# The first query products of finished token tiles placed at the end of the output projection's block, and the second query group's rounding with them

## The reference

```python
y = hybrid_mixer(h, ...)                       # ends in: merged @ w_out
x = x + gate1 * rms_norm(y, g_post_mix[l])
h = rms_norm(x, g_pre_ffn[l]) * (1.0 + scale2) + shift2
...
qry = (h @ w_query).reshape(T, P_HEADS, 2, P_HALF)          # T = 512, w_query is 1024 x 2048
scores = jnp.einsum("thcd,hcnd->thcn", qry, sub_keys)
s_top, i_top = lax.top_k(scores, P_TOPK)
```

## Time and profile before

| | us |
|---|---|
| three runs, median (lowest to highest) | 2040.17 (2038.8 to 2041.48) |
| the profiled execution | 2043.64 |
| its span, first to last instruction | 2041.9 |
| TensorE busy | 1950.5, 96% |
| VectorE busy | 1495.0, 73% |
| ScalarE busy | 720.0, 35% |
| GpSimd busy | 607.7, 30% |

### The profile page before, as it was taken

How to read it: one execution, slowest core, us unless ns; L and a number is a source line. 1 busy time by engine, 2 the same in 40 slices (tenths; PEclk the granted TensorE clock), 3 DMA queues, 4 the chain that set the end, 5 groups by cost and what they waited for, 6 DMA issues and landing times.

```text
span 2041.9 us, 27960 instructions
## 1 busy us (share of the span) xinstructions
PE 1950.5 (96%) x10317; PEld 1721.8 (84%) x10317; DVE 1495.0 (73%) x2721; ACT 720.0 (35%) x1324; POOL 607.7 (30%) x364
## 2 busy tenths in 40 slices
PE   5999998999999979999999999999999999999996
PEld 3889776889877868899999999999978888788885
DVE  5677545364475536777889999997688988788993
ACT  4010234010252243344443444444444444344442
POOL 0343402343203113101113732223433333343420
PEclk9999998999999989999999999999999999999998
DMA  6335411354212422257777688888999999999991
GB/s 249 103 104 185 165 51 40 100 202 144 62 42 76 151 83 75 74 171 252 232 225 256 222 314 305 305 303 308 411 379 394 396 396 397 396 397 396 391 346 68
DMA packets 230643, 468.00 MB, mean 229 GB/s; under 512 B 15576, under 2 KB 159120, under 8 KB 227728
## 3 DMA queue, kind: packets, MB, share of 16 engines
q1 hardware_dynamic: 193680, 332.54, 46.5%
q0 software_dynamic: 36864, 134.23, 17.4%
HBM read 412.19 MB, written 54.53 MB: 229 GB/s over the span
## 4 chain that ended last, share of the span: by engine, by line
PE 39%; DMA 10%; DVE 6%; issue 1%; ACT 1%; SPq 0%; POOL 0%; POOLq 0%; ACTq 0%; DVEq 0%
PE xin_ps_u L1946 23%; PE xin_out L1995 13%; DMA experts_hot<-act_scratch 8%; PE xin_out L1968 4%; DMA con_raw<-in_expert_u 1%; DVE over_v_vlo L2249 1%; DVE experts_acc L1765 1%; DVE experts_rows L1745 1%; DVE xin_wt L2246 1%; DVE in_ulo L2083 1%; DMA act_scratch<-in_act 0%; DVE xin_wlo L2251 0%; ACT in_uhi L2006 0%; SPq L1919 0%; DVE over_s_stage L2097 0%
## 5 line engine op out<-in xcount | busy, mean ns | idle before, releaser
L1946 PE MATMUL xin_ps_u<-con_h_hi,in_uhi 128*128 128x384 f32 x1024 | 348.0, 340 | 7.8 <-DVE in_ulo L2083 5.6
L1946 PE MATMUL xin_ps_u<-con_h_lo,in_uhi 128*128 128x384 f32 x1024 | 342.4, 334 | 0.0
L1946 PE MATMUL xin_ps_u<-con_h_hi,in_ulo 128*128 128x384 f32 x1024 | 342.4, 334 | 0.0
L1735 POOL DMA_INDIRECT experts_rows<-in_expert_rows,experts_idx x128 | 164.9, 1288 | 442.9 <-DVE experts_rows L1745 320.1
L1738 POOL DMA_INDIRECT experts_rows<-in_expert_v,experts_idx x128 | 201.9, 1578 | 313.7 <-DVE experts_acc L1765 297.3
L1995 PE MATMUL xin_out<-over_v_vhi,xin_whi 128*128 128x512 f32 x768 | 237.6, 391 | 8.6 <-DVE xin_wlo L2251 8.5
L476 POOL TENSOR_TENSOR weights_wlo<-con_raw,weights_whi 128x2048 fp32r<-128x2048 f32 x34 | 156.6, 4607 | 271.2 <-DVE weights_whi L537 271.2
L1995 PE MATMUL xin_out<-over_v_vlo,xin_whi 128*128 128x512 f32 x768 | 237.0, 390 | 0.0
L1995 PE MATMUL xin_out<-over_v_vhi,xin_wlo 128*128 128x512 f32 x768 | 236.8, 390 | 0.0
L2083 DVE TENSOR_TENSOR in_ulo<-con_raw,in_uhi 128x1024 fp32r<-128x1024 f32 x127 | 155.3, 1222 | 74.7 <-ACT in_uhi L2006 72.1
L1946 PEld LDWEIGHTS xin_ps_u<-con_h_hi,in_uhi 128*128 128x128 f32 x1024 | 192.4, 188 | 12.1 <-DVE in_ulo L2083 9.3
(11 more groups left out here) (330 smaller groups left out, 3819.1 us busy)
## 6 DMA issues: line engine op xcount, KB each, us to landing
con_raw<-in_expert_u SPq DMA_DIRECT2D x128, 512.0 KB, 5.1
con_raw<-in_expert_v SPq DMA_DIRECT2D x128, 512.0 KB
con_raw<-in_w_in SPq DMA_DIRECT2D x38, 1024.0 KB, 5.8
act_scratch<-in_act SPq DMA_DIRECT2D x128, 192.0 KB
experts_hot<-act_scratch SPq DMA_DIRECT2D x128, 192.0 KB
gate_scratch<-in_stage SPq DMA_DIRECT2D x12, 1024.0 KB
gate_scratch<-over_s_stage SPq DMA_DIRECT2D x12, 1024.0 KB
experts_hot<-gate_scratch SPq DMA_DIRECT2D x16, 768.0 KB
```

Of the source, the lines that this page charges most:

```text
L1735: pool.indirect_dma_start(out=self.rows[:, r % ROWS, 0:D], out_offset=None, in_=u_table, in_offset=at).then_inc(self.u_row_in[r % ROWS], 16)
L1946: mm = pe.matmul(ps_u[s % 2][:, 0:TD], a[s % 2][:, k, :], m[:, k, P:T], start=(i == 0), stop=(i == 3 * KD - 1))
```

## The change

Group 0 of the queries is cut by tokens. At the end of `finish_block`, TensorE computes both of its units for tiles 0 and 1 (256 tokens, `first_queries(slice(0, 2 * P))`) between the turns of tiles 2 and 3, and for tile 2 (128 tokens) behind the turn of tile 3. Only tile 3 (128 tokens) is left for `group(0)` in `query_block`. The two banks of PSUM go over from the one block to the other. Group 1 is rounded in `finish_block`, too: the high part by ScalarE in front of `modulate(3)`, the low part by GpSimd as its last instruction there; both are gone from `query_block`, whose counts of `w_hi` and `w_lo` are one lower, and the load of group 3 waits for nothing now.

```diff
@@ finish_block, gpsimd, behind the eight powers
+            pool.wait_ge(w_hi, 5)
+            pool.tensor_tensor(slots.wlo[1][:], raw[1][:], as_f32(slots.whi[1][:]), ALU.subtract).then_inc(query_lo, 1)
@@ finish_block, tensor
+            def first_queries(some):
+
+                for c in range(2):
+                    cs, i = slice(c * P, (c + 1) * P), 0
+                    for k in range(KD):
+                        for a, m in ((slots.whi, hi), (slots.whi, lo), (slots.wlo, hi)):
+                            pe.matmul(bank[c][:, some], a[0][:, k, cs], m[:, k, some], start=(i == 0), stop=(i == 3 * KD - 1))
+                            i += 1
+
             turn(2)
+            pe.wait_ge(w_lo, 4)
+            pe.wait_ge(low_done, 4)
+            for b in range(2):
+                pe.wait_ge(freed[b], U // 4)
+            first_queries(slice(0, 2 * P))
             turn(3)
+            pe.wait_ge(low_done, 6)
+            first_queries(slice(2 * P, 3 * P))
@@ finish_block, scalar
-                dst = w_hi_of[n] if n < 4 else slots.whi[0]
-                if n == 4:
-                    act.wait_ge(units, units_of.index((3, 0)) + 1)
+                dst = w_hi_of[n] if n < 4 else slots.whi[n - 4]
+                if n >= 4:
+                    act.wait_ge(units, units_of.index((3, n - 4)) + 1)
                 act.activation(dst[:], raw[n % 2][:], ACT.Copy).then_inc(w_hi, 1)
...
             modulate(2)
             square_tile(3)
+            split_hi(5)
             modulate(3)
@@ query_block, sync
-                wait(sp, w_lo, g - 2)
+                wait(sp, w_lo, g - 3)
...
-                sp.wait_ge(w_lo, PH - 2 + m // 2)
+                sp.wait_ge(w_lo, PH - 3 + m // 2)
@@ query_block, gpsimd
-            for g in range(1, PH):
-                pool.wait_ge(w_hi, g)
+            for g in range(2, PH):
+                pool.wait_ge(w_hi, g - 1)
@@ query_block, tensor
-                if g > 0:
-                    pe.wait_ge(w_lo, g)
+                if g > 1:
+                    pe.wait_ge(w_lo, g - 1)
+                some = slice(3 * P, T) if g == 0 else slice(0, T)
...
-                            mm = pe.matmul(bank[b][:], a[s][:, k, cs], m[:, k, :], start=(i == 0), stop=(i == 3 * KD - 1))
+                            mm = pe.matmul(bank[b][:, some], a[s][:, k, cs], m[:, k, some], start=(i == 0),
+                                           stop=(i == 3 * KD - 1))
@@ query_block, scalar
-                if g + 1 < PH:
+                if 0 < g < PH - 1:
```

More of the change, by code:

```diff
@@ L1235, in finish_block @@
              "stored"))
+        query_lo = al.sem("query_lo")
         pow_at = lambda kind, t: NORMS.index((kind, t)) + 1
@@ L1461, in _ @@
                         rounded(t)
+    return bank[0:2]
 class Consts:
@@ L1516, in mixer @@
         af.sb("m", [P, 2 * KD, T])
-        finish_block(nc, con, slots, A, m_hl, y, x_rows, late_w, x, x1, *hT)
+        return finish_block(nc, con, slots, A, m_hl, y, x_rows, late_w, x, x1, *hT)
 class Ring:
@@ L1597, with query_block @@
 PIECES, LATE_HEADS = 4, 2
-def query_block(nc, con, slots, ring, A, hT, qry, keys, rt, uhi, ulo, cut_hi, cut_lo):
+def query_block(nc, con, slots, ring, A, hT, qry, keys, rt, uhi, ulo, cut_hi, cut_lo, begun):
     with Alloc(nc, "query") as al:
@@ L1607, in query_block @@
         keys_t = al.sb("keys_t", [P, HC, NK])
-        bank = [al.ps(f"bank{i}", [P, T]) for i in range(4)]
+        begun_home = [al.ps(f"begun{i}", [P, T]) for i in range(2)]
+        bank = begun + [al.ps(f"bank{i}", [P, T]) for i in range(2)]
         ps = [al.ps(f"ps{i}", [P, 4, NK]) for i in range(4)]
@@ L2283, in _, with experts @@
                     dve.tensor_tensor(x[:, t + 1, half], x[:, t + 1, half], yg[m % 4][:], ALU.add).then_inc(dve_sum, 1)
-def experts(nc, con, slots, ring, A, hT, x1, acts, gmat, out):
+def experts(nc, con, slots, ring, A, hT, x1, acts, gmat, out, begun):
     with Alloc(nc, "over_s") as av:
@@ L2305, in experts @@
             qry = got.rows[:].rearrange("p a n -> p (a n)").rearrange("p (c t) -> p c t", t=T)
-            query_block(nc, con, slots, ring, A, hT, qry, hot[0:2], rt, uhi, ulo, cut_hi, cut_lo)
+            query_block(nc, con, slots, ring, A, hT, qry, hot[0:2], rt, uhi, ulo, cut_hi, cut_lo, begun)
             stage.append(stage1)
@@ L2327, in build_program @@
             head_block(nc, con, slots, A, A["x"].rearrange("b s d -> (b s) d"), *hT)
-            mixer(nc, con, slots, A, hT, x1)
+            begun = mixer(nc, con, slots, A, hT, x1)
         ring = Ring(al, slots)
-        experts(nc, con, slots, ring, A, hT, x1, acts, gmat, out.rearrange("b s d -> (b s) d"))
+        experts(nc, con, slots, ring, A, hT, x1, acts, gmat, out.rearrange("b s d -> (b s) d"), begun)
 NAMES = ["x", "c", "w_ada", "b_ada", "g_pre_mix", "g_post_mix", "g_pre_ffn", "g_post_ffn", "w_in", "b_if", "conv_w",
```

## The result

Five runs of each kernel, side by side on one chip: 2040.71 us before (2038.80 to 2043.27), 2049.49 us after (2047.08 to 2050.35). The ratio is 1.0040, 95% interval 1.0029 to 1.0052: slower by 8.2 us, 5.9 to 10.6. The forecast was 2050.6 and "slower".

A forecast was written before the change was run, and what follows sets the result against it. TensorE was taken to bound the kernel, with stops of 5.1 and 3.1 us and a lowered clock at the seam. 8.0 + 2.4 = 10.4 us slower, added to the median 2040.17, gave 2050.6; range 2037.5 to 2053.5.

The forecast's parts named there:

- Steps 1 and 2: Old block: 48 products of 256 columns take 5.8 us, to 747.1; then tile 3's turn at full clock, 1.9 us.
- The moved rounding: Old block: GpSimd's 4.6 us subtraction, ready at 746.85, gets in behind VectorE's tile 2 subtraction or cast, blocking VectorE until 751.6-752.0.
- step 3: Behind the turn of tile 3: TensorE waits for rounded tile 2, ready at 752.5 instead of 748.1.
- Step 4: Behind the turn of tile 3: TensorE stops from 749.0 to 752.5, some 3.4 us, and the clock falls.
- the stop at 1490: TensorE's stop of at least 3 us at 1490, which did not drop the clock; cited for the clock staying up.
- Steps 5 and 6: Tiles 2 and 3: 48 products each, 10.6 us at lower clock; query block 10.6 later, group 0's end 8.0 late.
- Step 7: Key transposes and group 1 start at the lower clock: 4.8 us of it cost 2.4 us.
- two records per narrow product: Rival: a 128-column product costs 0.236 us, 48 take 11.3; group 0 ends 11.8 us late, 2052.0; chance 0.13.
- Clock falls but rises within the narrow products: Rival: VectorE blocked, clock rises after 4.8 us within the 128-column products; 0.7 us late, 2040.9; chance 0.22.
- no block: Rival: GpSimd gets in only after 748.14, or not at VectorE's cost; 4.9 us sooner, 2035.3; chance 0.11.
- clock stays: Rival: VectorE blocked, but the clock stays up behind the stop; 1.6 us sooner, 2038.6; chance 0.09.
- hidden edits: Query block: group 3's early load behind the keys, costed at nothing; 3.6 us if transfers shared evenly and nothing hid it.

The follow-up runs named there:

- e1: The changed kernel with GpSimd's subtraction of group 1 and the load of group 3 back in the query block; -4.7 us against before, ratio 0.9972 to 0.9990.
- e2: The changed kernel with group 1's subtraction on VectorE behind its last rounding instead of on GpSimd; -4.8 us against before, ratio 0.9970 to 0.9990.
- e7: The changed kernel with GpSimd's subtraction of group 1 cut into four at the same place; -3.6 us against before, ratio 0.9969 to 0.9988.
- e3: The changed kernel with 15 unread 512-column products filling the stop behind the turn of tile 3; -1.8 us against before, ratio 0.9985 to 1.0003.
- e5: e4 with GpSimd's subtraction of group 1 back in the query block; -7.5 us against before, ratio 0.9945 to 0.9971.
- e8: The changed kernel with both of group 1's roundings back in the query block, only products moved; -5.3 us against before, ratio 0.9964 to 0.9986.
- e4: The changed kernel with tiles 2 and 3 done together as 256-column products in the query block; -3.0 us against before, ratio 0.9979 to 0.9996.
- e6: e1 with the keys' transposes moved between the two halves of group 1's products; -6.4 us against before, ratio 0.9953 to 0.9979.
- e9: e5 with the stop filled by 15 unread products and the keys' transposes between group 1's halves; -7.4 us against before, ratio 0.9952 to 0.9979.

## Why the prediction was right

By its steps, all counted from the turn of tile 2:

- **Steps 1 and 2** (first products, turn of tile 3): the turn started at 8.34 us, forecast 8.2, and took 1.95 at full clock. The 48 products of 256 columns took 5.83 us, 0.12 each.
- **The moved rounding and step 3**: GpSimd started 7.88 us behind the mark (forecast 7.9), got in at the end of the first of the two instructions named, and tile 2 was ready at 13.58 (forecast 13.6). e1, e2 and e7 show that it is this instruction and its length that does it.
- **Step 4**: a stop of 3.35 us (forecast 3.4), and the clock fell. The prediction assumed this. That the stop brings the fall is shown by e3 (stop filled, 1.00 throughout) and e5 (a stop of 3.6 us with no narrow products behind it, and the clock fell). But such a stop does not always do it, and the case against, the stop at 1490, was weaker than it looked: the same stop, 3.34 to 3.35 us long, stands in all eleven profiles, and behind it the clock fell in eight and stayed at 1.00 in three, the kernel before among them. In the changed kernel (stop from 1492.20 to 1495.55) it fell there, too:

```profile
1492.00:1495.00 3.00, 0.20 (x2) 0.00 (x0) 1.41 (x3) 1.84 (x3) 0.94 (x1) 1.00 1.03 408
1496.00:1498.00 2.00, 2.00 (x6) 1.54 (x6) 0.47 (x1) 0.81 (x1) 0.00 (x0) 0.50 1.04 419
```

- **Steps 5 and 6**: the narrow stream did not raise the clock. A narrow product at the lower level measured 0.214 us (48 in 10.28), not 0.22, and the clock fell only 1.7 us into the stream, so that some 15 of them still ran at 0.112. The block switch came 8.9 us later than before (forecast 10.6), the transposes of the keys 6.0 later (forecast 8.0). 15 x 0.108 + 81 x 0.006 is 2.1 us, which covers the miss of 2.0 at the transposes.
- **Step 7**: mis-sized. The clock came back at the end of the transposes, not 4.8 us after they began, so they cost 1.3 us more than before instead of 2.4. The sum is 6.0 + 1.3 = 7.3 where the prediction had 8.0 + 2.4 = 10.4; 7.3 is below its own bounds of 9.0 to 12.2, which had no place for a clock that falls late.
- **The total** was nearer (+8.8 by medians, +8.2 by the ratio, 5.9 to 10.6) than the sum, by scatter of the runs, not by merit.

The rivals: two records per narrow product are out (the trace has one record for each narrow product, and at full clock 16 of them in e1 start between 746.28 and 747.96, 0.112 us apart; the prediction had 0.115). Half as many columns go hardly faster than 256 (0.12). The page TensorE: Matmul & The Clock Gate (Trainium skill, LDWEIGHTS (loading the stationary operand)) gives a load's ns as its columns over 1.2, by which an estimate for 128 is 107 ns: the trace's 0.112 us per product at full clock stands near that (at the lower level it is 0.214), and far from the 81 ns per product that the same page has (Back-to-back issue gap), which the prediction turned down. "Clock falls but rises within the narrow products" fell with the changed kernel's own windows; "no block" and "clock stays" did too. Their prices held where an experiment made them true: e1 is "no block" (forecast 4.9 us faster, measured 4.7) and e3 is "clock stays up" (forecast 1.6 us faster, measured 1.8, with an interval that reaches no difference).

Of the hidden edits: the early load of group 3 behind the keys cost little, if anything. With it the wait for the keys ended 6.6 (e2), 6.0 (e3) and 6.4 us (e7) after the block start, with the old order 6.3 (e1) and 6.0 us (e8).

## What to carry to other kernels

When work is moved to an idle engine, look at what it locks for the others while it runs, not only at whether the engine is free: a 4.7 us GpSimd instruction beside short VectorE roundings on the critical path made one of them, 0.42 us alone, last 4.74 us. With the same work elsewhere none was lengthened, and in four pieces each by about 1 us. A stop of TensorE of some 3.4 us can cost more in the clock behind it than in itself (8.9 against 3.4 us here), though a stop of that length did not drop the clock every time. It cost most where narrow products followed it; so keep the wide products for the place behind a stop, or fill it. And compare two executions from a mark ahead of the change, since this profile's lead of 3.0 us from earlier stages would have hidden nearly half of the loss.

## What the hardware did that I had not expected

- **When the clock falls.** In the four executions in which it fell at this seam it did so 3.1 us (before), 5.0 us (after), 5.0 us (e4) and 4.0 us (e5) after TensorE's last product. The stops were 5.1, 3.35, 5.7 and 3.6 us long: in two of the four it fell only when TensorE was already working again, 1.7 and 0.4 us into the next stream. With stops of 1.06 us or less at this seam (e1, e2, e3, e6 to e9) it did not fall in any profile. One and the same stop of 3.35 us between the two expert passes was followed by a fall in eight of eleven profiles, 2.0 to 4.6 us after TensorE's last product, and by none in three (before, e1, e5). So the length of a stop does not decide it alone; what else does is open.
- **What brings it back.** 512-column products did after 4.8 us (before), 256-column ones after 6.1 (e4) and 3.8 us (e5), 128-column ones not within 17.9 us (after), though they kept it at 1.00 for 11 us when it had not fallen (e1). It rose 2.6 us into the key transposes, which are 128 columns wide too; the turn of tile 3 before, of the same kind and 3.8 us long, had not raised it. Why the transposes did and the narrow products did not is open: no run here takes the two apart.
- **Two engines in turns.** With short pieces GpSimd and VectorE alternate strictly (e7): each instruction of VectorE waited for one piece of GpSimd, about 1 us, and not for the rest of them.
